# The experts' down slabs issued from ScalarE's DMA queue, up slabs kept on SyncE's

## The chip, the cores and the metric

The kernel runs on one core of a Trainium2 chip. The metric is device time in microseconds (us), the median of several runs. A profile is one further execution, recorded by the hardware profiler. Engines are named as the profile names them: PE is TensorE (matmuls), PEld its weight loads, DVE VectorE, ACT ScalarE, POOL GpSimd and SP SyncE. SPq and ACTq are the queues from which SyncE and ScalarE issue transfers.

## The reference

Two blocks of two layers each, all in float32, on 256 tokens of width 1024. The first block mixes the tokens (attention, Fourier, gates) and then sends them through 16 experts, of which each takes the 32 tokens that score highest for it. In layer 0 this is done for two token sets (the latents and the context), in layer 1 for the latents alone.

```
def expert_choice_ffn(h, w_router, w_gate_e, w_up_e, w_down_e):
    B, N, _ = h.shape
    cap = CAPACITY_FACTOR * N // N_EXPERTS
    aff = jax.nn.softmax((h @ w_router).astype(jnp.float32), axis=-1)
    top_aff, top_idx = lax.top_k(aff.transpose(0, 2, 1), cap)
    ...
    a = jnp.einsum("becd,edf->becf", xg, w_gate_e)
    u = jnp.einsum("becd,edf->becf", xg, w_up_e)
    out = jnp.einsum("becf,efd->becd", jax.nn.silu(a) * u, w_down_e) * top_aff[..., None].astype(h.dtype)
    return jnp.zeros_like(h).at[bidx, top_idx].add(out)
```

Each expert has three matrices of 1024 x 1024 floats (4 MB each), so the 32 expert passes read 32 x 12 MB of weights. The second block (three kinds of attention and a cross attention, two layers) has no experts.

## The kernel before

All weights go through one ring in SBUF, `ring`, with four slots of 2 MB (`RING = 4`). `slab_plan` lists the slabs in the order in which TensorE uses them. For an expert these are six: parts 0 to 3 ("up slabs") hold two row blocks of w_gate_e and two of w_up_e, in two transfers of 1 MB; parts 4 and 5 ("down slabs") hold four row blocks of w_down_e each, in one transfer of 2 MB. `loads` gives the transfers of a slab. An engine program is written by hand for each engine, and an engine runs its instructions in that order.

SyncE walks through the whole plan (line 711 on). Before slab i it waits until `slab_used` has reached i - 3, that is, until the slab that lay in the same slot has been used; then it issues the transfers, which count up the slot's semaphore. TensorE waits for that semaphore (`slab_wait`), multiplies, and counts up `slab_used` (`last_release`, line 840).

In `experts` TensorE does, for each expert, the four up slabs (line 1109; in layer 0 for two token sets, `ns = 2`, in layer 1 for one). Then come, from the fifth expert on, matmuls that add earlier results to the tokens (line 1093). Then it turns the product (line 1123), which needs ScalarE's copy of the up product out of PSUM (line 1391). ScalarE's sigmoid (line 1396) and VectorE's products (lines 1840, 1845) must be done before the two down slabs (line 1136). Behind the first down slab TensorE gathers rows for a later group of experts (line 1015), which ScalarE copies (line 1354); behind the second it turns weights (line 1026), which ScalarE copies too (line 1360). ScalarE's own program for an expert is: copies of the up product, sigmoids, row copies, weight copy. It issues transfers only at the start of the kernel (line 1443), 0.16 MB in all.

Of the kernel before, what the change touches and what calls it, by code (L numbers as in the profile page):

```python
# [33 lines left out]
RING = 4  # L34
# [90 lines left out]
def signal(name):  # L125

    if name in SHARED:
        return SHARED[name]
    base = name.replace("@0", "").replace("@1", "")
    return base, LAYER0[base] if "@1" in name else 0  # L130
# [8 lines left out]
def build(nc, a, out, ctx):  # L139
# [5 lines left out]
    def sem(name):  # L145
        name = signal(name)[0]
        if name not in sems:
            sems[name] = ctx.enter_context(nc.semaphore(name))
        return sems[name]
# [95 lines left out]
    def slot(i):  # L245
        return ring[:, (i % RING) * SLAB:(i % RING + 1) * SLAB]

    plan = slab_plan()
    where = {p: i for i, p in enumerate(plan)}

    def kcol(w, n0, n):
        return w.rearrange("(k p) n -> p k n", p=P)[:, :, n0:n0 + n]

    def loads(kind, l, s):

        if kind == "ada":
            return [(0, KC, COL, kcol(a["w_ada"][l], s * COL, COL))]
        if kind == "expert":
            e, part = s // 6, s % 6
            if part < 4:  # L260
                return [(c0, 2, D, a[name][l, e].rearrange("(k p) n -> p k n", p=P)[:, 2 * part:2 * part + 2, :])
                        for c0, name in ((0, "w_gate_e"), (2 * D, "w_up_e"))]
            return [(0, 4, D, a["w_down_e"][l, e].rearrange("(k p) n -> p k n", p=P)[:, 4 * (part - 4):4 * (part - 4) + 4, :])]
        if kind == "qkv":
            return [(0, KC, COL, kcol(a["w_in"][l], s * COL, COL))]
        if kind == "gate":
            return [(0, KC, COL, kcol(a["w_in"][l], MIX + (s % 3) * D + (s // 3) * COL, COL))]
        if kind == "branch":
            return [(0, 2, COL, kcol(a["w_br_fourier"][l], s * COL, COL)),
                    (2 * COL, 4, COL, kcol(a["w_br_global"][l], s * COL, COL)),  # L270
                    (6 * COL, 2, COL, kcol(a["w_br_window"][l], s * COL, COL))]
        if kind == "out":
            return [(0, KC, COL, kcol(a["w_out"][l], s * COL, COL))]
        if kind == "in2":
            return [(0, KC, COL, kcol(a["w_in_2"][l], s * COL, COL))]
        if kind == "out2":
            return [(0, KC, COL, kcol(a["w_out_2"][l], s * COL, COL))]
        if kind == "xq":
            return [(0, KC, COL, kcol(a["w_xq_2"][l], 0, COL))]
        if kind == "xkv":  # L280
            return [(0, KC, COL, kcol(a["w_xkv_2"][l], s * COL, COL))]
        return [(0, 4, D, kcol(a["w_xo_2"][l], 0, D))]
# [16 lines left out]
    slab_used = sem("slab_used")  # L299
# [411 lines left out]
    @block.sync  # L711
    def _(sp):
        for i, (kind, l, s) in enumerate(plan):
            if i >= RING:
                sp.wait_ge(slab_used, i - RING + 1)
            for c0, k, n, src in loads(kind, l, s):
                sp.dma_start(slot(i)[:, c0:c0 + k * n].rearrange("p (k n) -> p k n", k=k), src
                             ).then_inc(sem(f"slab_landed{i % RING}"), 16)
        sp.wait_ge(*at("result", 2))
        for t in range(2):  # L720
            sp.dma_start(out[0, t * P:(t + 1) * P, :], X[:, t, :]).then_inc(sem("stored"), 16)
        sp.wait_ge(*at("stored", 32))
# [517 lines left out]
    def _(act):  # L1240
# [71 lines left out]
        def experts(l):  # L1312
            ns = 2 - l
            order = tile_order(l)
            place = order.index
            turn_of = set_order(l).index
            log_and_exp()

            def square(t):
                n = place(t) + 1  # L1320
                act.wait_ge(*at(f"x_mid@{l}", n))
                act.activation(XN[:, t, :], X[:, t, :], ACT.Square, accum_out=st[:, SS + t:SS + t + 1]
                               ).then_inc(sem(f"n2@{l}_sq"), 1)
                act.wait_ge(*at(f"n2@{l}_var", n))
                act.activation(st[:, RS + t:RS + t + 1], st[:, VAR + t:VAR + t + 1], ACT.Ln
                               ).then_inc(sem(f"n2@{l}_ln"), 1)
                act.wait_ge(*at(f"n2@{l}_ln", n))
                act.activation(st[:, RS + t:RS + t + 1], st[:, RS + t:RS + t + 1], ACT.Exp, scale=-0.5
                               ).then_inc(sem(f"n2@{l}_rs"), 1)

            def modulated_tile(t):
                act.wait_ge(*at(f"n2@{l}_t0", place(t) + 1))
                s = t // 2
                for k in range(4):
                    ins = act.activation(HT[:, k, t * P:t * P + P], ps[6 if t == 3 else 4][:, k * P:(k + 1) * P], ACT.Identity,
                                         scale=SCL[:, l, 1, k, s:s + 1], bias=MODT[:, l, 24 + k, s:s + 1])
                ins.then_inc(sem(f"n2@{l}_ht0"), 1)

            def exps(s):
                act.wait_ge(*at(f"rmax@{l}", turn_of(s) + 1))  # L1340
                for t in range(2):
                    ins = act.activation(affinities(s)[:, t, :], ps[2 * s][:, t * E:(t + 1) * E], ACT.Exp,
                                         bias=soft_stat("neg", s)[:, t:t + 1],
                                         accum_out=soft_stat("sum", s)[:, t:t + 1])
                ins.then_inc(sem(f"rexp@{l}"), 1)

            pieces = [0]

            def rows_in(g, s, h):
                pieces[0] += 1  # L1350
                act.wait_ge(*at(f"gathered@{l}", pieces[0]))
                for kk in range(4):
                    k = 4 * h + kk
                    ins = act.activation(XGT[:, s, k, g * P:(g + 1) * P], ps[6 + h][:, kk * P:(kk + 1) * P], ACT.Identity,
                                         scale=SCL[:, l, 1, k, s:s + 1], bias=MODT[:, l, 24 + k, s:s + 1])
                ins.then_inc(sem(f"xgt@{l}"), 1)

            def weights_in(g, s, b, n):
                act.wait_ge(*at(f"gw_turned@{l}", n))
                act.activation(GW[:, s, g, :], ps[b][:, 0:SEQ], ACT.Copy).then_inc(sem(f"gw@{l}"), 1)  # L1360

            if l == 0:
                square(2)
                square(3)
                act.wait_ge(*at(f"mod@{l}", 2))
                modulated_tile(2)
                modulated_tile(3)
                exps(1)
            square(0)
            modulated_tile(0)  # L1370
            square(1)
            modulated_tile(1)
            exps(0)
            act.preload_act_table(ACT.Sigmoid)
            if l == 0:
                rows_in(0, 1, 0)
                rows_in(0, 1, 1)
            for m in range(2 * ns):
                act.wait_ge(*at(f"gmm@{l}_1", m + 1))
                act.activation(GB[:, m // 2, m % 2 * COL:(m % 2 + 1) * COL], ps[2 + m % 2][:, :], ACT.Copy  # L1380
                               ).then_inc(sem(f"grow@{l}_1"), 1)
            rows_in(0, 0, 0)
            rows_in(0, 0, 1)
            turned = 0
            for e in range(E):
                for s in range(ns):
                    m = e * ns + s
                    act.wait_ge(*at(f"up_done@{l}", m + 1))
                    if e:
                        act.wait_ge(*at(f"gu_turned@{l}", m - ns + 1))  # L1390
                    act.activation(GU[:, s, :], ps[s][:, :], ACT.Copy).then_inc(sem(f"gu_read@{l}"), 1)  # L1391
                for s in range(ns):
                    m = e * ns + s
                    act.wait_ge(*at(f"gu_turned@{l}", m + 1))
                    gate = ps[2 + s][:, :].rearrange("p (c n) -> p c n", c=4)[:, :, 0:2 * CAP]
                    act.activation(EG[:, s], gate, ACT.Sigmoid).then_inc(sem(f"eg@{l}"), 1)
                if e < 12:
                    for s, h in gather_pieces(l, e % 4):
                        rows_in(e // 4 + 1, s, h)
                if weight_set(l, e % 4) >= 0:  # L1400
                    turned += 1
                    weights_in(e // 4, weight_set(l, e % 4), 7 - e % 2, turned)
# [659 lines left out]
```

## Time and profile before

| | us |
|---|---|
| median of 3 runs | 2778.69 (2778.27 to 2779.12) |
| time of the profiled execution | 2783.78 |
| its span, first to last instruction | 2781.9 |
| PE busy | 2188.0 (79%) |
| PEld busy | 1056.5 (38%) |
| DVE busy | 737.7 (27%) |
| ACT busy | 455.0 (16%) |
| mean granted TensorE clock | 0.878 |
| TensorE in the experts of layer 0 | 645.45 to 1135.57 in the trace |
| TensorE in the experts of layer 1 | 1466 to 1947.67 in the trace |

The page divides the span into 40 slices of 69.5 us and gives for each the busy share of an engine in tenths, the granted TensorE clock and what the DMA engines moved. A share over the whole span is a mean of stages with different limits, so the stages have to be read one by one: by windows, by the order of instructions in time, and by what an engine waited for. In the order of time a row is a start, a duration and an operation; the number in brackets is how long the engine had been idle, and for what.

### The profile page before, as it was taken

The numbers are of one execution on the slowest core, as the hardware profiler recorded it, in microseconds if no ns is written. First come the engines' busy times: TensorE is split into PE (matmuls) and PEld (weight loads), VectorE is DVE, ScalarE is ACT, GpSimd is POOL, SyncE is SP. The second block draws the span as 40 slices with busy tenths as digits, with TensorE's granted clock in tenths as the row PEclk, the third lists the DMA queues.
The fourth block names the chain that finished last, engine by engine and source line by source line (L and its number), as shares of the span: only waits on it lengthen the run. The fifth ranks groups of instructions, "written<-read, shape, count | busy, mean of one in ns | idle before, by whom it ended". The sixth has DMA issues, their size and how long they took to land.

```text
span 2781.9 us, 30472 instructions
## 1 busy us (share of the span) xinstructions
PE 2188.0 (79%) x12882; PEld 1056.5 (38%) x12882; DVE 737.7 (27%) x1873; ACT 455.0 (16%) x1097; POOL 22.9 (1%) x44
## 2 busy tenths in 40 slices
PE   4997999888888888798976655555697679896686
PEld 3444544454333333354442121111244434334433
DVE  1030720342222222334140011111304731115622
ACT  1011700012101110115011000000103411013302
POOL 2000000000000000000000000000000000000000
PEclk8999999989999999999987798878896579995588
DMA  9136036416999999531328999999441022340010
GB/s 299 61 127 237 1 111 222 182 61 262 408 409 408 407 405 409 220 114 54 121 91 354 409 409 409 409 409 407 162 141 44 1 76 91 121 151 1 16 61 23
DMA packets 187333, 577.30 MB, mean 208 GB/s; under 512 B 7392, under 2 KB 7856, under 8 KB 187200
## 3 DMA queue, kind: packets, MB, share of 16 engines
q1 hardware_dynamic: 183936, 567.31, 52.9%
q0 software_dynamic: 2800, 7.89, 1.0%
q8 instruction: 104, 1.70, 0.3%
q14 instruction: 29, 0.24, 0.0%
q10 hardware_dynamic: 464, 0.16, 0.0%
HBM read 574.28 MB, written 1.05 MB: 207 GB/s over the span
## 4 chain that ended last, share of the span: by engine, by line
PE 36%; DMA 25%; issue 16%; DVE 8%; PEld 8%; PEldq 4%; ACT 3%; SPq 1%; POOL 0%; DVEq 0%; POOLq 0%
PE ps L831 16%; DMA ring<-w_up_e 15%; DMA ring<-w_down_e 7%; PEld ps L831 4%; PEldq L841 3%; PE ps L964 3%; PE ps L1109 2%; PEld ps L1136 2%; PE ps L921 2%; DMA ring<-w_ada 2%; PE ps L424 1%; DMA ring<-w_in 1%; PE ps L514 1%; PE ps L412 1%; PE ps L533 1%
## 5 line engine op out<-in xcount | busy, mean ns | idle before, releaser
L831 PE MATMUL ps<-ring,reg_a 128*128 128x512 f32 (+1 forms) x1632 | 710.7, 595 | 18.8 <-issue 8.2
L1109 PE MATMUL ps<-ring,reg_bc 128*32 128x512 f32 x3072 | 414.3, 678 | 181.9 <-DMA ring<-w_up_e 173.7
L831 PEld LDWEIGHTS ps<-ring,reg_a 128*128 128x128 f32 x1632 | 312.1, 193 | 412.8 <-issue 397.9
L1109 PEld LDWEIGHTS ps<-ring,reg_bc 128*32 128x32 f32 x3072 | 95.3, 117 | 476.2 <-DMA ring<-w_up_e 277.4
L1136 PE MATMUL ps<-ring,reg_bc 128*32 128x256 f32 x3072 | 182.8, 386 | 74.0 <-issue 42.7
L1136 PEld LDWEIGHTS ps<-ring,reg_bc 128*32 128x32 f32 x3072 | 104.1, 111 | 138.3 <-issue 55.6
L1827 DVE TENSOR_TENSOR reg_e<-ps,reg_e 128x512 f32<-128x512 f32 x48 | 33.0, 687 | 454.7 <-PE ps L1093 454.7
L1516 DVE COPY reg_bc<-ps 128x512 f32<-128x512 f32 (+1 forms) x33 | 22.3, 675 | 445.3 <-PE ps L831 445.3
L1391 ACT ACTIVATE reg_bc<-ps 128x512 f32<-128x512 f32 x48 | 28.7, 597 | 657.0 <-PE ps L1109 657.0
L1855 DVE COPY reg_a<-ps 32x256 f32<-32x256 f32 x192 | 80.7, 420 | 205.8 <-PE ps L1136 203.3
L412 PE MATMUL ps<-ident,tmp 128*128 128x128 f32 x160 | 50.3, 414 | 73.7 <-DVE tmp L635 47.4
L1269 ACT ACTIVATE reg_bc<-ps 128x512 f32<-128x512 f32 (+1 forms) x33 | 19.3, 584 | 440.7 <-PE ps L831 440.7
L921 PE MATMUL ps<-ring,reg_d 128*128 128x512 f32 x192 | 85.0, 603 | 4.0 <-DMA ring<-w_br_window 2.9
L964 PE MATMUL ps<-ring,reg_a 128*128 128x512 f32 x192 | 86.1, 607 | 1.8 <-DVE reg_e L1649 1.6
L814 PE MATMUL ps<-ident,reg_d 128*128 128x128 f32 x160 | 41.3, 413 | 54.9 <-DVE reg_d L1499 51.4
L797 PE MATMUL ps<-ring,ct 128*32 128x128 f32 x1536 | 53.4, 296 | 30.9 <-DMA ring<-w_ada 27.3
L424 PE MATMUL ps<-reg_bc,tmp 128*128 128x64 f32 (+1 forms) x320 | 70.8, 375 | 0.0
L424 PEld LDWEIGHTS ps<-reg_bc,tmp 128*128 128x128 f32 x320 | 70.1, 305 | 0.6
L412 PEld LDWEIGHTS ps<-ident,tmp 128*128 128x128 f32 x160 | 22.9, 193 | 114.4 <-DVE tmp L635 57.8
L1269 ACT ACTIVATE reg_e<-ps 128x512 f32<-128x512 f32 x36 | 21.5, 597 | 264.0 <-PE ps L831 263.9
L403 PE MATMUL ps<-reg_e 64*128 64x256 f32 (+1 forms) x128 | 60.3, 612 | 2.5 <-ACT reg_e L1418 0.9
L797 PEld LDWEIGHTS ps<-ring,ct 128*32 128x32 f32 x1536 | 46.0, 120 | 39.4 <-DMA ring<-w_ada 28.9
(276 smaller groups left out, 1982.1 us busy)
## 6 DMA issues: line engine op xcount, KB each, us to landing
ring<-w_gate_e SPq DMA_DIRECT2D x128, 1024.0 KB, 13.4
ring<-w_up_e SPq DMA_DIRECT2D x128, 1024.0 KB, 16.3
ring<-w_down_e SPq DMA_DIRECT2D x64, 2048.0 KB, 16.7
ring<-w_in SPq DMA_DIRECT2D x34, 2048.0 KB, 8.7
ring<-w_ada SPq DMA_DIRECT2D x24, 2048.0 KB, 15.7
ring<-w_out SPq DMA_DIRECT2D x8, 2048.0 KB, 8.5
ring<-w_xkv SPq DMA_DIRECT2D x4, 2048.0 KB, 7.8
ring<-w_br_global SPq DMA_DIRECT2D x4, 1024.0 KB, 8.0
```

The lines of the kernel that those rows point to most:

```text
L403: mm = pe.matmul(score_bank(i)[:, 0:u["nk"]], u["q"], u["k"], start=True, stop=True)
L412: mm = pe.transpose(ps[2 + j % 2][:, c * P:c * P + P], S2[j % 2][:, c * P:c * P + P], ident[:, :])
L424: mm = pe.matmul(ps[4 + j % 2][:, 0:w], PT[j % 2][:, c * P:c * P + P], u["v"][c], start=(c == 0), stop=(c == n - 1))
L797: mm = pe.matmul(ps[6 + s % 2][32 * j:32 * j + 32, 0:P], CT[:, k, :], w[:, k, j * P:j * P + P], start=(k == 0), stop=(k == KC - 1))
L814: mm = pe.transpose(ps[4 + 2 * s + k % 2][:, t * P:t * P + P], src[:, 2 * s + t, k * P:k * P + P], ident[:, :])
L831: mm = pe.matmul(ps[b][:, c0:c1], lhs(t, k), w[:, k, c0:c1], start=(q == 0), stop=(q == len(chunks) - 1))
L841: pe.drain().then_inc(slab_used, 1)
L921: mm = pe.matmul(ps[4 + n % 4][:, :], OT[:, k, t * P:t * P + P], w[:, k, :], start=(k == k0), stop=(k == k1 - 1))
L964: mm = pe.matmul(ps[t][:, :], HT[:, k, t * P:t * P + P], w[:, k, :], start=(k == 0), stop=(k == KC - 1))
L1109: mm = pe.matmul(ps[s][32 * j:32 * j + 32, :], XGT[:, s, 2 * q + k, e * CAP:(e + 1) * CAP], w[:, j // 2, k, (j % 2) * COL:(j % 2 + 1) * CO ...
L1136: mm = pe.matmul(ps[4 + s][32 * j:32 * j + 32, 0:SEQ], HE[:, s, k, q * CAP:(q + 1) * CAP], w[:, k, j * SEQ:(j + 1) * SEQ], start=(q == 0 a ...
L1855: ins = dve.tensor_copy(OE[r:r + CAP, e // 4 % 2, s, j * SEQ:(j + 1) * SEQ], ps[4 + s][CAP * j:CAP * (j + 1), 0:SEQ])
```

## The change

SyncE leaves out parts 4 and 5 of every expert. ScalarE issues them, at the head of its program for that expert, each behind a wait for the same count of `slab_used`. Slots, semaphores and sizes stay as they are.

```
     def _(sp):
         for i, (kind, l, s) in enumerate(plan):
+            if kind == "expert" and s % 6 >= 4:
+                continue
             if i >= RING:
                 sp.wait_ge(slab_used, i - RING + 1)
...
             rows_in(0, 0, 1)
             turned = 0
             for e in range(E):
+                for part in (4, 5):
+                    i = where[("expert", l, 6 * e + part)]
+                    act.wait_ge(slab_used, i - RING + 1)
+                    for c0, k, n, src in loads("expert", l, 6 * e + part):
+                        act.dma_start(slot(i)[:, c0:c0 + k * n].rearrange("p (k n) -> p k n", k=k), src
+                                      ).then_inc(sem(f"slab_landed{i % RING}"), 16)
                 for s in range(ns):
                     m = e * ns + s
                     act.wait_ge(*at(f"up_done@{l}", m + 1))
```

SyncE's queue at the end of layer 1's experts, before the change: the last up slabs, the two down slabs of the last expert, and the first slabs of the second block (w_in_2).

```order
L717 DMA ring<-w_gate_e 128x2x1024 [waits slab_used]
L717 DMA ring<-w_up_e 128x2x1024
L717 DMA ring<-w_gate_e 128x2x1024 [waits slab_used]
L717 DMA ring<-w_up_e 128x2x1024
L717 DMA ring<-w_down_e 128x4x1024 [waits slab_used] x2
L717 DMA ring<-w_in_2 128x8x512 [waits slab_used] x8
```

The same place after it (the line is now 719):

```order
L719 DMA ring<-w_gate_e 128x2x1024 [waits slab_used]
L719 DMA ring<-w_up_e 128x2x1024
L719 DMA ring<-w_gate_e 128x2x1024 [waits slab_used]
L719 DMA ring<-w_up_e 128x2x1024
L719 DMA ring<-w_in_2 128x8x512 [waits slab_used] x8
```

The two down transfers are gone from this queue, and the next stage's slabs follow the up slabs directly; at the end of each earlier expert the next expert's up slabs do.

ScalarE's queue in the experts of layer 0, before: two copies of the up product (`up_done`), two sigmoids, the row copies, the weight copy, and the next expert's copies.

```order
L1391 ACTIVATE reg_bc<-ps 128x512 [waits gu_turned,up_done] x2
L1396 ACTIVATE reg_bc<-ps 128x256 [waits gu_turned] x2
L1354 ACTIVATE reg_bc<-ps,modt,scl 128x128 [waits gathered]
L1354 ACTIVATE reg_bc<-ps,modt,scl 128x128 x3
L1360 ACTIVATE reg_e<-ps 128x256 [waits gw_turned]
L1391 ACTIVATE reg_bc<-ps 128x512 [waits gu_turned,up_done] x2
```

The same place after it (1391 is now 1399, 1396 is 1404, 1354 is 1356, 1360 is 1362):

```order
L1399 ACTIVATE reg_bc<-ps 128x512 [waits gu_turned,up_done] x2
L1404 ACTIVATE reg_bc<-ps 128x256 [waits gu_turned] x2
L1356 ACTIVATE reg_bc<-ps,modt,scl 128x128 [waits gathered]
L1356 ACTIVATE reg_bc<-ps,modt,scl 128x128 x3
L1362 ACTIVATE reg_e<-ps 128x256 [waits gw_turned]
L1392 DMA ring<-w_down_e 128x4x1024 [waits slab_used] x2
L1399 ACTIVATE reg_bc<-ps 128x512 [waits gu_turned,up_done] x2
```

The two issues stand between the weight copy of one expert and the up product's copies of the next, each with its wait for `slab_used`.

## Rows read from the trace of the kernel before

**Rows 1.** The page's 40 slices: DMA busy in tenths, and the rate.
```profile
DMA  9136036416999999531328999999441022340010
GB/s 299 61 127 237 1 111 222 182 61 262 408 409 408 407 405 409 220 114 54 121 91 354 409 409 409 409 409 407 162 141 44 1 76 91 121 151 1 16 61 23
```
**Rows 2.** The page's queues (packets, MB, share) and issues (KB, us to landing).
```profile
q1 hardware_dynamic: 183936, 567.31, 52.9%
...
ring<-w_down_e SPq DMA_DIRECT2D x64, 2048.0 KB, 16.7
```
**Rows 3.** DMA views of 680 to 1120 us, and then of 1480 to 1940 us.
```profile
DMA packets 45970, 179.43 MB, mean 408 GB/s; under 512 B 2266, under 2 KB 2266, under 8 KB 45934
...
DMA packets 48288, 188.20 MB, mean 409 GB/s; under 512 B 2399, under 2 KB 2399, under 8 KB 48267
```
**Rows 4.** PE in order of time, one expert of layer 1.
```profile
1806.29 1.92 PE L1109 MATMUL ps<-ring,reg_bc 128*32 128x512 f32 x16 [1.88 <-DMA ring<-w_up_e]
1811.39 3.25 PE L1109 MATMUL ps<-ring,reg_bc 128*32 128x512 f32 x16 [3.18 <-DMA ring<-w_up_e]
...
1818.37 1.93 PE L1136 MATMUL ps<-ring,reg_bc 128*32 128x256 f32 x32 [1.90 <-issue]
1821.90 1.93 PE L1136 MATMUL ps<-ring,reg_bc 128*32 128x256 f32 x32 [1.59 <-DMA ring<-w_down_e]
```
**Rows 5.** SyncE's issues in order of time, one up slab of the same expert.
```profile
1823.94 0.37 SPq L717 DMA_DIRECT2D ring<-w_gate_e  x1
1824.35 2.31 SPq L717 DMA_DIRECT2D ring<-w_up_e  x1
```
**Rows 6.** PE in order of time, one expert of layer 0.
```profile
941.22 3.66 PE L1136 MATMUL ps<-ring,reg_bc 128*32 128x256 f32 x64 [1.93 <-issue]
...
947.19 3.66 PE L1136 MATMUL ps<-ring,reg_bc 128*32 128x256 f32 x64
951.14 11.13 PE L1109 MATMUL ps<-ring,reg_bc 128*32 128x512 f32 x96 [0.29 <-issue]
963.17 3.64 PE L1109 MATMUL ps<-ring,reg_bc 128*32 128x512 f32 x32 [0.90 <-DMA ring<-w_up_e]
...
971.97 3.66 PE L1136 MATMUL ps<-ring,reg_bc 128*32 128x256 f32 x64 [1.94 <-issue]
```
**Rows 7.** The chain that ended last, at the end of either layer's experts.
```profile
1119.46 3.64 PE ps L1109 x32
...
1945.69 1.98 PE ps L1136 x32
```
**Rows 8.** DMA view of 0 to 30 us; windows of 4 to 16, 36 to 48 us.
```profile
GB/s 0 0 71 137 360 410 418 421 401 396 390 397 376 375 372 403 369 388 390 391 391 382 353 324 166 27 87 46 169 158 275 244 166 109 89 163 255 240 384 363
...
q0 software_dynamic: 1579, 3.60, 49.6%
q1 hardware_dynamic: 2167, 4.37, 43.4%
...
ring<-w_ada SPq DMA_DIRECT2D x4, 2048.0 KB, 33.4
...
4.00:16.00 12.00, 0.89 (x6) 0.48 (x10) 0.67 (x4) 1.94 (x3) 12.00 (x22) 1.00 1.05 392
36.00:48.00 12.00, 6.92 (x134) 5.52 (x130) 0.94 (x5) 0.00 (x0) 0.00 (x0) 0.77 1.05 387
```
**Rows 9.** The chain around 772 us, and a window there (last: clock, DMA share, GB/s).
```profile
772.54 5.34 PE ps L1109 x32
...
773.00:774.00 1.00, 1.00 (x12) 0.36 (x8) 0.00 (x0) 0.00 (x0) 0.00 (x0) 0.52 1.03 410
```
**Rows 10.** Whom ScalarE waited for, in total, times, longest.
```profile
ACT reg_bc L1391 <- PE ps L1109: 657.0, 48, 29.5
```
**Rows 11.** SyncE's first issues for layer 0's experts, and the window behind them.
```profile
649.17 4.11 SPq L717 DMA_DIRECT2D ring<-w_down_e  x2
...
650.00:660.00 10.00, 9.79 (x92) 2.62 (x84) 0.00 (x0) 0.60 (x1) 0.00 (x0) 1.00 0.96 372
```

More of the change, by code:

```diff
@@ L713, in _ @@
         for i, (kind, l, s) in enumerate(plan):
+            if kind == "expert" and s % 6 >= 4:
+                continue
             if i >= RING:
@@ L1385, in experts @@
             for e in range(E):
+                for part in (4, 5):
+                    i = where[("expert", l, 6 * e + part)]
+                    act.wait_ge(slab_used, i - RING + 1)
+                    for c0, k, n, src in loads("expert", l, 6 * e + part):
+                        act.dma_start(slot(i)[:, c0:c0 + k * n].rearrange("p (k n) -> p k n", k=k), src
+                                      ).then_inc(sem(f"slab_landed{i % RING}"), 16)
                 for s in range(ns):
```

## The prediction

> **What bounds the kernel now.** I read the slices of the page first: two stretches of about 480 us, the experts of layer 0 and of layer 1, in which the DMA digit is 9 and the rate stays at 405 to 409 GB/s [rows 1]. The DMA view of each stretch says the same: 408 and 409 GB/s with one queue, q1, doing nearly all of it [rows 2, 3]. A slab is 2048 KB [rows 2] or 2.097 MB, so it takes 2.097 / 0.409 = 5.13 us, and an expert (six slabs) 30.8 us. In layer 1 TensorE starts on the slabs as they land: up slabs at 1806.29 and 1811.39, the second down slab at 1821.90, each start with a wait for DMA before it [rows 4]. In layer 0 TensorE has two token sets and is close to the bound too. From the start of the fourth up slab at 963.17 its loop is 8.80 us to the first down slab, 5.97 to the second, 3.95 to the next expert's first up slab, 11.13 for three up slabs, and some 0.3 of gaps: 30.2 us against 30.8 [rows 6]. So both stages are bound by bytes, with 0.6 us of room per expert in layer 0.
>
> What I call U0 to U3 are an expert's up slabs, D0 and D1 its down slabs. A slab is issued when the one four places ahead has been used: D0 when U0 is used, D1 at U1, the next expert's U0 at U2.
>
> **What the change removes, adds and moves.** No byte, matmul or activation goes. 64 transfers of 2 MB leave SyncE's queue for ScalarE's, with a wait for the same count of used slabs. SyncE never was the limit: an issue takes it 0.37 us, against 5.13 us per slab, though a second one can be held for 2.31 us when much is outstanding [rows 5]. Taking work from it gives 0.
>
> ScalarE gets 64 issues, 64 x 0.37 = 24 us if they cost there what they cost SyncE. ScalarE sat idle 657.0 us in front of the 48 copies of line 1391, waiting for matmuls [rows 10]. It blocks on the use of U0 and then of U1. Behind it in its queue stand the copies that wait for U3, two slabs or at least 7.4 us later, and the row and weight copies of the expert before, which stand ahead of the issues, wait for matmuls that TensorE runs before U0. So issue times hardly move, and even a hold of 2.3 us would be over before U3 has been used. Cost 0. If that cover were gone, 2.3 us x 32 experts = 74 us would be the bound.
>
> What changes is the **order in which the bytes are served**. Before, one queue serves slabs in the order in which they are used. Afterwards the down slabs stand in a queue of their own beside the up slabs. The only place in the trace where two queues are busy together is the start: in the first 30 us the software queue took 49.6% of the engines' time and q1 43.4%, and the first four 2 MB slabs took a median of 33.4 us to land [rows 8]. Neither queue waited until the other was empty; they shared about evenly. The total was not changed: 392 GB/s in 4 to 16 us with both, against 387 for q1 alone on rows of the same 2 KB in 36 to 48 us [rows 8]. I take an equal share for SyncE's and ScalarE's queues; their pair is not in this trace, so both extremes are rivals below.
>
> The page "DMA: Bandwidth & Descriptors" of the Trainium skill says in "Queues, rings and completion order" that each DMA engine goes round between its queue rows packet by packet; the rows above agree with that. By its section "Issuing engines are not separate DMA queues" alone, which says only that the transfers interleave on the same 16 engines and that issue time is saved, the sum would be 0.
>
> Take U0's landing as time 0 in layer 1. In the order of use the landings are 0, 5.1, 10.3, 15.4 (U3), 20.5 (D0), 25.6 (D1), 30.8 (next U0). With equal shares D0 arrives when U2 is nearly served; U3 then has half the bandwidth for its whole service and lands at 10.7 + 10.3 = 21.0, with D0 just ahead of it. D1 then shares with the next U0 and both are in at about 30.3 to 30.8. The next U1 has the engines to itself. So the period stays 30.8 us, but **U3 and D1 are in about 5 us later than in the order of use**, and the place of what they lose is taken by slabs that are not needed yet. Inside the run that costs nothing while the DMA engines have work, since they set the pace. It is paid once, at the end of each stage, where slabs of the next stage have been served ahead of D1.
>
> *Layer 1.* D1 of the last expert starts at 1945.69 and ends at 1947.67 [rows 7]. U3 landed 10.3 earlier, 1935.4. Afterwards U3 is at 1940.5; 6.98 us to D0 [rows 4], 2.3 to D1 and 1.93 for it give 1951.7. By D1's own landing, 1945.7 + 4.7 + 1.98 = 1952.3. Cost 4.6, between 0 (order of use) and 9.2 (both down slabs wholly ahead of U3).
>
> *Layer 0.* The end follows U3 of the last expert, 1119.46, by a chain of matmuls, not D1's landing [rows 7]. U3 is 5.1 later in the first experts; of this the TensorE loop of 30.2 against 30.8 gives nothing back, since the engines are still the pace, but TensorE late means slabs issued late. I take 4.5, between 0 and 5.1 for this term.
>
> *A thin margin in layer 0.* At U3's landing 9.8 us of D1 and next U0 and 5.1 us of U1 are unserved, 14.9 us. The next issue, U2, comes when D0 is used, 8.80 + 3.66 = 12.5 us later, and some 1.4 us pass until it moves bytes (an estimate: the first issue is at 649.2 and the rate then reads 372 GB/s over 650 to 660 us [rows 11]): 13.9. So the DMA engines stay busy with 1.0 us to spare. The waits for U3 grow to 4 or 5 us, and after a wait of 2.71 us at 772.54 that slab's matmuls took 5.34 instead of 3.64 us while the granted clock read 0.52, close to the lower of its two levels, 1.2 of 2.4 GHz [rows 9]. That is 1.7 us more than the margin allows by 0.7, so 16 x 0.7 = 11 us if it came at each expert. A late TensorE does not wait, and then keeps its clock, so I take 2 us, between 0 and 11.
>
> In layer 1 TensorE has 10 us of room per expert and its fourth slab already runs 3.25 us, most of it at half clock [rows 4]; 0. Everything outside the experts has the same queue as before: 0; slabs served early for the next stages are not waited for there, 0 to -1.
>
> Sum: 4.6 + 4.5 + 2 = +11. On the profiled execution, 2783.78 us (span 2781.9), that is 2795; the median of the runs is 5.1 lower, so 2778.7 + 11.1 = 2790.
>
> **The rivals.**
> 1. *Order kept.* The queues serve the older transfer first, or the descriptors come through one place in order. For it: long holds of the second issue on SyncE, up to 2.3 us here [rows 5], show that something behind the issue fills up. Against: the shared start [rows 8]. Then nothing moves: 2779. A late ScalarE, so that D0 is issued only when it is needed, would belong here as "the change does not do what it says", but its idle time [rows 10] speaks against it.
> 2. *Unequal shares.* If ScalarE's queue gets clearly more than half, U3 waits for D0 and D1. At the extreme only 10.3 us are unserved when U3 lands, against 13.9 needed, so the DMA engines stand still 3.6 us per expert of layer 0: 58 us, plus 10 and 9 at the ends, 2856. The point from which this decides is the 1.0 us of margin. With less than half for ScalarE's queue D0 and D1 come late instead, with a like loss. The starting shares of 49.6 to 43.4 are near equal, so I price the case at a third of the extreme: 2800 to 2820.
> 3. *Faster.* Two queues keep the engines better filled. For it: single slices of the first 30 us read up to 421 GB/s [rows 8] where one queue holds 409; against: slices that follow read 376, and the stretch as a whole 392. If 3% held, layer 1 would win 14 us and layer 0, held by the loop of 30.2, 16 x 0.6 = 9; less 11 for the order: -12, 2767. It decides from 2% more bandwidth on (-10 and -9 against +11).
>
> **How the numbers follow.** Forecast (equal shares, 2784 to 2797) 0.52, predicted 2790. Order kept 0.22 (2776 to 2782). Unequal 0.17 (2797 to 2830, a tail beyond). Faster 0.09 (2765 to 2773). About 0.2%, 5.6 us, is what a measurement of this kernel can tell from no change, so the bounds are 2773 and 2784. Slower: 0.52 less 0.03 on its edge, plus 0.17, 0.66. Same: 0.22 + 0.03, 0.25. Faster: 0.09. The range of 2776 to 2808 leaves out the faster case and the upper half of the unequal one.
>
> **What would show it.** In the profile of the changed kernel: q10 with some 134 MB; 409 GB/s in both stretches; down slabs landing before or with U3; in layer 1 a wait of 7 to 10 us in front of U3 and next to none in front of D0 and D1; ScalarE's copies of line 1391 late only by U3; experts' stretches 5 us longer each. Waits in front of each slab as even as before would show order kept; gaps in the DMA rate in layer 0 would show rival 2; a rate over 412 GB/s rival 3. I am wrong above all if the two queues do not share evenly.

## The result, and the profile after

The changed kernel takes 2793.43 us (median; 2786.11 to 2799.22), the kernel before 2778.89 us beside it. The ratio is 1.0049, 95% interval 1.0037 to 1.0062: 14.5 us slower. The prediction was 2790, slower by 11.

The profiled execution has a span of 2791.1 us. Its slices and queues, which answer to [rows 1] and [rows 2]:

```profile
DMA  9136035416999999531328999999441022340010
GB/s 298 64 138 221 1 114 218 181 61 270 408 405 409 391 408 396 216 120 61 108 103 317 408 409 409 409 404 408 168 151 60 0 75 91 119 142 11 15 60 23
...
q1 hardware_dynamic: 150144, 433.08, 40.6%
q10 hardware_dynamic: 34256, 134.39, 12.1%
...
ring<-w_down_e ACTq DMA_DIRECT2D x64, 2048.0 KB, 15.8
```

ScalarE's queue is q10, and it carries the 134 MB. In the experts of layer 0 two slices read 391 and 396 GB/s where all read 405 to 409 before. The next windows run from the first up matmul to the last down matmul of each layer, of the kernel before and then of the changed one (length, busy times, granted clock, DMA share, GB/s):

```profile
645.45:1135.57 490.12, 416.06 (x4478) 179.24 (x4478) 111.76 (x252) 52.10 (x119) 0.00 (x0) 1.00 1.01 403
1466.28:1947.67 481.39, 281.27 (x2238) 91.24 (x2238) 55.78 (x124) 25.85 (x59) 0.00 (x0) 0.81 1.02 406
```
```profile
646.20:1145.10 498.90, 423.58 (x4478) 180.74 (x4478) 111.70 (x252) 52.09 (x119) 0.00 (x0) 0.98 1.01 398
1477.00:1962.70 485.70, 267.50 (x2238) 92.00 (x2238) 55.80 (x124) 25.85 (x59) 0.00 (x0) 0.80 1.02 404
```

Layer 0 is 8.8 us longer, layer 1 4.3 us, 13.1 together. The two spans differ by 9.2 only, since the rest was 3.9 us shorter this time. What is left of the span, the same work in all kernels, came out between 1800 and 1812 us from one profiled execution to the next. So I judge the experiments by these two windows as well as by the medians. The windows of the kernel with all issues on ScalarE, below, came within 1 us of those before. With two queues a window repeats less well: the four rows of the table below in which layer 1 has the changed kernel's program give 485.7, 486.2, 487.9 and 489.9 us there.

One expert of layer 1 after the change, answering to [rows 4] (TensorE in order of time):

```profile
1810.20 3.95 PE L1111 MATMUL ps<-ring,reg_bc 128*32 128x512 f32 x32 [0.29 <-issue]
1818.01 3.61 PE L1111 MATMUL ps<-ring,reg_bc 128*32 128x512 f32 x16 [3.86 <-DMA ring<-w_up_e]
1828.41 3.53 PE L1111 MATMUL ps<-ring,reg_bc 128*32 128x512 f32 x16 [6.78 <-DMA ring<-w_up_e]
...
1835.68 1.93 PE L1138 MATMUL ps<-ring,reg_bc 128*32 128x256 f32 x32 [1.91 <-issue]
1838.18 1.93 PE L1138 MATMUL ps<-ring,reg_bc 128*32 128x256 f32 x32 [0.57 <-DMA ring<-w_down_e]
```

U0 and U1 run without a wait between them, U2 lands at 1818.01 and U3 10.40 us after it. That is a slab at half the rate: 10.3 us was the figure. Then the down slabs are nearly there. The queues' shares in 1816 to 1817 us (packets, MB, share of the engines):

```profile
q10 hardware_dynamic: 50, 0.20, 51.1%
q1 hardware_dynamic: 49, 0.20, 50.5%
```

**Where the DMA engines stand still.** In layer 0 some windows lose bytes. First two windows of 30 us; then, from the first of them, TensorE's rows for a U3 and a D0, and SyncE's issue of the next U2:

```profile
910.00:940.00 30.00, 26.70 (x288) 11.87 (x284) 7.52 (x16) 3.21 (x8) 0.00 (x0) 1.00 0.95 366
1060.00:1090.00 30.00, 23.27 (x244) 9.59 (x248) 7.53 (x16) 1.96 (x4) 0.00 (x0) 0.89 0.97 378
```
```profile
906.02 5.34 PE L1111 MATMUL ps<-ring,reg_bc 128*32 128x512 f32 x32 [3.84 <-DMA ring<-w_up_e]
916.52 3.66 PE L1138 MATMUL ps<-ring,reg_bc 128*32 128x256 f32 x64 [1.94 <-issue]
...
920.25 0.37 SPq L719 DMA_DIRECT2D ring<-w_gate_e  x1
```

U3 waited 3.84 us, then ran at the lower clock, 5.34 us instead of 3.64; D0 was used at 920.2, and only then could the next U2 be issued. The rate read 289 GB/s in 918 to 920 us and 145 in 920 to 922. Against 409 GB/s, 30 us at 366 are (409 - 366) / 409 x 30 = 3.2 us of standing still, 30 us at 378 are 2.3, and a window of 30 us from 820 on with 402 gives 0.5, 6.0 together. In the second window it is the same: U3 waited 6.53 us and took 5.23 at 1063.86, and the rate read 277 and 127 GB/s in 1076 to 1080, around the issue of a U2 at 1077.88. By the same sum the kernel before loses 0.8 us.

**The end of the stage.** The last U3 of layer 0 and of layer 1, answering to [rows 7]:

```profile
1126.20 6.48 PE L1111 MATMUL ps<-ring,reg_bc 128*32 128x512 f32 x32 [3.32 <-DMA ring<-w_up_e]
...
1951.87 3.24 PE L1111 MATMUL ps<-ring,reg_bc 128*32 128x512 f32 x16 [7.08 <-DMA ring<-w_up_e]
...
1958.85 3.97 PE L1138 MATMUL ps<-ring,reg_bc 128*32 128x256 f32 x64 [1.90 <-issue]
```

In layer 0 U3 starts 480.0 us after the stage's first matmul; before it was 474.0 (1119.46 - 645.45). It then takes 6.48 us instead of 3.64: 6.0 + 2.8 = 8.8, all of the lengthening. In layer 1 U3 starts 474.9 us in, 5.7 later than before (1935.46 - 1466.28 = 469.2), and both down slabs run in one piece behind it without a wait for DMA. In this execution D1's landing is not what the end waits for. In two others, whose program for layer 1 is the same, TensorE did wait for it. These are the rows of the last D1 in the changed kernel's repetition and in the changed kernel with five more matmuls:

```profile
1954.37 1.94 PE L1138 MATMUL ps<-ring,reg_bc 128*32 128x256 f32 x32 [1.87 <-DMA ring<-w_down_e]
```
```profile
1965.02 3.64 PE L1142 MATMUL ps<-ring,reg_bc 128*32 128x256 f32 x32 [6.00 <-DMA ring<-w_down_e]
```

In the second of them the last U3 started 472.3 us in, only 3.1 later than before, and the stage took 489.9 us all the same. So the end of layer 1 has two ways to be late, U3's and D1's, and which one is taken changed from one profiled execution to the next.

### The profile page after: what moved, and what is told of

Same layout as the page of the kernel before. It is cut to its first block, busy times and chain, and to the rows that moved or that the text cites. A ratio compares the mean times of both kernels' runs of the same rounds, so it can differ in the third digit from the quotient of the medians.

```text
span 2791.1 us, 30472 instructions
## 1 busy us (share of the span) xinstructions
PE 2177.4 (78%) x12882; PEld 1057.7 (38%) x12882; DVE 737.5 (26%) x1873; ACT 454.8 (16%) x1097; POOL 22.9 (1%) x44
## 3 DMA queue, kind: packets, MB, share of 16 engines
HBM read 574.28 MB, written 1.05 MB: 206 GB/s over the span
## 4 chain that ended last, share of the span: by engine, by line
PE 40%; DMA 22%; issue 16%; DVE 8%; PEld 8%; PEldq 3%; ACT 3%; SPq 1%; POOL 0%; DVEq 0%; POOLq 0%; ACTq 0%
PE ps L833 16%; DMA ring<-w_up_e 13%; DMA ring<-w_down_e 6%; PE ps L1111 4%; PEld ps L833 4%; PE ps L966 3%; PEldq L843 3%; PE ps L923 2%; PEld ps L1138 2%; DMA ring<-w_ada 2%; PE ps L424 1%; DMA ring<-w_in 1%; PE ps L1138 1%; PE ps L514 1%; PE ps L412 1%
## 5 line engine op out<-in xcount | busy, mean ns | idle before, releaser
L1111 PE MATMUL ps<-ring,reg_bc 128*32 128x512 f32 x3072 | 403.7, 663 | 205.0 <-DMA ring<-w_up_e 190.4
L1111 PEld LDWEIGHTS ps<-ring,reg_bc 128*32 128x32 f32 x3072 | 96.3, 117 | 483.0 <-DMA ring<-w_up_e 252.0
L1524 DVE COPY reg_bc<-ps 128x512 f32<-128x512 f32 (+1 forms) x33 | 22.3, 675 | 443.0 <-PE ps L833 443.0
L1399 ACT ACTIVATE reg_bc<-ps 128x512 f32<-128x512 f32 x48 | 28.7, 597 | 672.2 <-PE ps L1111 672.2
L1848 DVE TENSOR_TENSOR reg_bc<-reg_bc,ps 128x256 f32<-128x256 f32 x48 | 19.9, 414 | 158.2 <-ACT reg_bc L1404 158.2
```

The costliest lines, as they stand in the source:

```text
L1111: mm = pe.matmul(ps[s][32 * j:32 * j + 32, :], XGT[:, s, 2 * q + k, e * CAP:(e + 1) * CAP], w[:, j // 2, k, (j % 2) * COL:(j % 2 + 1) * CO ...
```

## The experiments

Theory at the start: U3 of the last expert lands late because down slabs are served beside it, and in layer 0 the DMA engines stand still now and then. Rivals: ScalarE's issuing or a second queue costs time as such; the cost comes equally with each expert; or slabs of the next stage take D1's place. These are the stages of each kernel, by the windows described above (us; the last column is the ratio of the medians to the kernel before on the same chip):

| kernel | layer 0 | layer 1 | ratio, 95% interval |
|---|---|---|---|
| before | 490.1 | 481.4 | |
| changed | 498.9 | 485.7 | 1.0049 (1.0037 to 1.0062) |
| changed, once more | 498.7 | 486.2 | 1.0042 (1.0028 to 1.0056) |
| one queue, U3 and D0 swapped everywhere | 594.2 | 491.3 | 1.0402 (1.0387 to 1.0416) |
| all slabs issued by ScalarE | 490.2 | 482.2 | 1.0016 (1.0007 to 1.0025) |
| last expert only | 499.2 | 488.4 | 1.0056 (1.0042 to 1.0069) |
| all but the last | 493.2 | 483.0 | 1.0009 (1.0000 to 1.0018) |
| one queue, swapped in the last expert | 496.3 | 485.7 | 1.0031 (1.0021 to 1.0042) |
| last expert only, next stage held back | 500.0 | 491.1 | 1.0059 (1.0047 to 1.0071) |
| before, sums of layer 0 left out | 487.8 | 481.6 | 0.9994 (0.9982 to 1.0005) |
| changed, sums of layer 0 left out | 493.9 | 487.9 | 1.0046 (1.0032 to 1.0061) |
| changed, five more matmuls | 503.9 | 489.9 | 1.0042 (1.0029 to 1.0056) |

### Does ScalarE's issuing cost anything?

```
+                i0 = where[("expert", l, 0)] + 6 * e + 4
+                for part in range(3):
+                    issue(i0 + part)
...
+                issue(i0 + 3)
+                issue(i0 + 4)
...
+                issue(i0 + 5)
```

`issue` waits for the slot and issues the slab's transfers. D0, D1 and the next U0 stand ahead of the copies of the up product, the next U1 and U2 behind the sigmoids, the next U3 ahead of the weight copy; SyncE skips them all.

> All slabs that follow an expert's first four, up and down and the first four of the next stage, are issued by ScalarE, in the order of use, so that one queue again holds everything; the issues stand at the points of its program where the slot comes free. Theory (order of service): the time of before, 2776 to 2782, with ScalarE issuing 320 transfers instead of 64. Rival (ScalarE's issuing, with its holds, delays the copies, or issues late): slower than the change, 2793 or more, with five times its issues.

Both stages are back at the times of before, 490.2 and 482.2 us, with five times as many issues on ScalarE:

```profile
q10 hardware_dynamic: 107856, 402.84, 36.4%
q1 hardware_dynamic: 76544, 164.63, 16.5%
...
645.20:1135.40 490.20, 414.38 (x4478) 178.85 (x4478) 111.77 (x252) 52.19 (x119) 0.00 (x0) 1.00 1.02 403
1466.00:1948.20 482.20, 280.19 (x2238) 90.02 (x2238) 55.81 (x124) 25.89 (x59) 0.00 (x0) 0.83 1.02 406
```

The rival falls: what matters is that one queue holds the slabs in order, not whose queue it is. The median, 2785.70 us, is 0.16% above before, which the two stages don't explain; it lies outside the 2776 to 2782 expected, and stays open.

### One queue with the order that sharing produces: a kernel that failed its purpose

```
+        order = list(range(len(plan)))
         for i, (kind, l, s) in enumerate(plan):
+            if kind == "expert" and s % 6 == 3:
+                order[i], order[i + 1] = i + 1, i
+        for i in order:
+            kind, l, s = plan[i]
```

> All slabs stay on SyncE's one queue, but the first down slab of each expert is issued ahead of the fourth up slab. No second queue and nothing on ScalarE; what is copied from the change is that the fourth up slab (U3) lands one slab, 5.1 us, later. Theory (the order in which the bytes are served is the cause): the change's cost comes back without its queue, 2786 to 2795 against 2779 before; in layer 1 about 4 us longer, with U3's wait grown to 6 to 8 us and the down slabs already there. Rival 1 (a second queue, or ScalarE's issuing, costs time as such): 2779. Rival 3 of the prediction has nothing to say here.

114 us slower, nearly all in layer 0 (594.2 us), and not for the reason under test. SyncE runs in order. With D0 ahead of U3, U3's issue stands behind D0's wait for the use of U0, although its own slot came free with the use of the D1 before:

```profile
900.66 0.37 SPq L722 DMA_DIRECT2D ring<-w_down_e  x1
901.07 0.51 SPq L722 DMA_DIRECT2D ring<-w_gate_e  x1
...
900.00:905.00 5.00, 4.78 (x48) 1.25 (x44) 0.00 (x0) 0.00 (x0) 0.00 (x0) 1.00 0.66 196
...
935.00:940.00 5.00, 4.89 (x46) 1.44 (x50) 1.33 (x4) 0.38 (x1) 0.00 (x0) 1.00 0.08 32
```

By then everything issued had been served (32 GB/s in 935 to 940 us). 104 us over 16 experts is 6.5 us each. So this kernel says nothing of the order; it shows what it costs when an issue that is due waits behind one that isn't.

The same swap in the last expert alone:

```
+            if kind == "expert" and s == 6 * E - 3:
+                order[i], order[i + 1] = i + 1, i
```

> One queue, SyncE's, and nothing on ScalarE. Only in the last expert of each layer the first down slab is issued ahead of the fourth up slab (U3). Other than in the kernel with the swap in every expert, the DMA engines have three slabs waiting when SyncE stands at the down slab's wait, so they do not run dry. Theory (a late U3 of the last expert is what the change's cost at the end of a stage consists of): 5 us later and about 2 us of slower clock in layer 0, 4 us in layer 1, 2788 to 2793. Rival (a second queue, or ScalarE, is needed for the cost): the time of before, 2779.

```profile
1120.68 5.44 PE L1114 MATMUL ps<-ring,reg_bc 128*32 128x512 f32 x32 [6.59 <-DMA ring<-w_up_e]
```

The stages are 6.2 us longer in layer 0 and 4.3 in layer 1, the latter the same as the change's, and the median of 2791.88 us lies in the range expected. A late U3 alone, with one queue and no issue on ScalarE, is enough for a cost of this size at the end.

### Once at the end, or with each expert?

```
-            if kind == "expert" and s % 6 >= 4:
+            if kind == "expert" and s % 6 >= 4 and s // 6 == E - 1:
```

and, the other way round, `s // 6 < E - 1`, with ScalarE's loop cut in the same way.

> Only the last of the 16 experts of each layer has its down slabs issued by ScalarE, 4 transfers in all. Theory (the reordering is paid once, at the end of a stage, where slabs of the next stage are served first and U3 lands late): nearly all of the end costs, 4.5 in layer 1 and 4 to 5 in layer 0, 2786 to 2789. Rival (a cost per expert, each 14.5 / 32 = 0.45 us): +0.9, 2780.

> All experts but the last of each layer have their down slabs issued by ScalarE. Theory: layer 1 as before to 0.5 us, although U3 waits 7 to 10 us in 15 experts; layer 0 keeps what the standing still of the DMA engines costs, 3 to 5 us; 2781 to 2785. Rival (a cost per expert): 15/16 of 14.5, 2792.

Four moved transfers of 64 cost all of it: ratio 1.0056. The other 60 cost 0.0009, and in layer 1, where U3 waits long in each of 15 experts, 1.6 us. A cost per expert is ruled out. The last expert alone was expected to cost 7 to 10 us and costs 16 (9.1 and 7.0 in the stages), a miss; the two parts add up to more than the change. Its U3s:

```profile
1120.77 5.84 PE L1111 MATMUL ps<-ring,reg_bc 128*32 128x512 f32 x32 [5.08 <-DMA ring<-w_up_e]
...
1947.22 3.64 PE L1111 MATMUL ps<-ring,reg_bc 128*32 128x512 f32 x16 [6.76 <-DMA ring<-w_up_e]
```

In layer 0 U3 starts 481.0 us in, 7.0 later than before, and takes 2.2 us more at the lower clock. That is later than half the rate allows: the shares in 1109 to 1117 us of this kernel are not equal.

```profile
q10 hardware_dynamic: 615, 2.45, 76.7%
q1 hardware_dynamic: 213, 0.82, 25.8%
```

In layer 1 it is alike: 69.4% for q10 and 33.4% for q1 in 1936 to 1942 us, U3 7.9 later than before.

In the changed kernel D0 of the last expert is issued at 1115.47, when TensorE is already late, and U3 lands 10.7 us later; here D0 is issued at 1102.37, 18.4 us ahead of U3. In the changed kernel the DMA engines had stood still 5.2 us more than before, and U3 was 6.0 late; here they stood still 0.6 us by the same sum, no more than before, and U3 was 7.0 late. So, as far as these two show, lateness from standing still and lateness from sharing stand in for each other: the later TensorE is, the less of the down slabs is served ahead of U3.

### Are slabs of the next stage to blame?

The kernel with the last expert only, and in SyncE's loop:

```
+            ends = [where[("expert", d, 0)] + 6 * E for d in range(DEPTH)]
+            if i in ends:
+                sp.wait_ge(slab_used, i)
+            elif i >= RING and i - 1 not in ends and i - 2 not in ends and i - 3 not in ends:
```

> As the kernel in which only the last expert of each layer has its down slabs issued by ScalarE, but SyncE holds the first four slabs of the next stage back until that expert's second down slab has been used. So no slab of the next stage is served before the last down slab. The prediction's step (the place of what the down slabs lose is taken by slabs not needed yet, and D1 lands late): most of the end cost of 15.7 us goes, 2782 to 2786. Second theory (the end cost is U3, late because D0 and D1 themselves are served beside it; D1's own landing is not waited for): nothing of it goes, 2792 to 2797.

Nothing goes: 2797.45 us, ratio 1.0059 against 1.0056, and neither stage is shorter (500.0 and 491.1 us against 499.2 and 488.4). SyncE issues the next slabs at 1143.74, when the stage is over, and U3 of layer 0 still lands late:

```profile
1125.58 5.57 PE L1114 MATMUL ps<-ring,reg_bc 128*32 128x512 f32 x32 [4.98 <-DMA ring<-w_up_e]
...
1143.74 10.36 SPq L722 DMA_DIRECT2D ring<-w_in  x4
```

That is 482.0 us into the stage, 8.0 late. So where the end follows U3, the step of the prediction that blamed the next stage's slabs falls; D0 and D1 themselves are what U3 is late for. TensorE waited for the last D1 in neither of these two kernels, so the pair says nothing of the executions in which it did. There the step may hold. In the kernel with five more matmuls q1 moved some 1.1 MB of the next stage's slabs in 1952 to 1960 us, beside D0 and D1, and 1.07 MB more in 1960 to 1964, while TensorE stood waiting for D1: 2.2 MB or 5.3 us at 409 GB/s (an estimate), against a wait of 6.00. Nobody held them back in that kernel.

### The margin in layer 0

Both the kernel before and the changed one are run once more without the sums of the first twelve experts in layer 0, that is, without four matmuls per expert ahead of the down slabs and without VectorE's part of them (not shown):

```
+                    if l == 0 and turn < 3:
+                        pe.sem_inc(sem(f"scatter@{l}"), 1)
+                        continue
```

> The kernel before, with the adding of the first twelve experts' results to the tokens left out in layer 0 (the four matmuls per expert of 1.96 us in all between the fourth up slab and the down slabs, from the fifth expert on, and VectorE's products and sums for them). The way from the fourth up slab to the use of the first down slab is about 2 us shorter. Layer 0 is bound by DMA in either theory, so only the last expert's 2 us are won there: its experts take 488 instead of 490 us.

> The changed kernel with the same left out. Theory (in layer 0 a margin of 1 us between the bytes that are unserved and the next issue decides whether the DMA engines stand still): with 2 us more margin the gaps in the DMA rate go, and layer 0 is longer than in the kernel before without these sums by the end cost alone, 5 to 7 us instead of 8.9. Rival (the dips have another cause, such as the two queues themselves): dips of the rate to 360 or less stay, 9 us.

The stages came out as expected, 487.8 and 493.9, a difference of 6.1 us. The gaps did not go: windows of 30 us in the second kernel read 389, 398, 377 and 381 GB/s, together 6.7 us of standing still. So this pair came out neither as the theory (no gaps) nor as the rival (9 us). The reason stands in TensorE's rows:

```profile
999.77 6.50 PE L1114 MATMUL ps<-ring,reg_bc 128*32 128x512 f32 x32 [4.87 <-DMA ring<-w_up_e]
```

With less to do, TensorE waits longer for U3 (4.87 us), and the matmuls behind the wait take 6.50 us instead of 3.64. From U3's start to the next issue of U2 it is 13.1 us (1012.86), 1.1 less than in the changed kernel's case above (14.2), not 2. So the prediction's account of the margin is not shown by this pair: the 2 us were partly given back by the clock, and whether a fixed margin of 1 us decides stays open. What the rows do show is that, in the places looked at, the rate drops around the issue of a U2 that waited for TensorE's late use of D0.

### The clock

```
+                    if q == 3 and e == E - 1 and l == 0:
+                        pe.wait_ge(*at(f"hid@{l}", e * ns))
+                        for _ in range(5):
+                            pe.matmul(ps[2][:, 0:COL], ident[:, :], mask[:, 0:COL], start=True, stop=True)
```

> The changed kernel, and in front of the wait for the last expert's fourth up slab (U3) in layer 0 TensorE runs five more matmuls of 128x512 (about 3 us, into a bank that nobody uses then; their result is not read). They fit into the wait of 3.3 us. Theory (of the 8.9 us in layer 0, 2.8 are U3's matmuls at the lower clock, 6.48 instead of 3.64 us, because of the wait before them): U3 takes 3.6 to 4 us, and layer 0's experts are 2 to 3 us shorter than in the changed kernel, although TensorE has more to do; in all 2 to 3 us less, too little to be told by the medians alone. Rival (the clock falls for another reason, or its cost lies beside other work): layer 0 as in the changed kernel or longer.

> The changed kernel once more, on the same chip as the one with the added matmuls, to see how far its stages repeat. Theory (late U3 at both ends plus the standing still of the DMA engines in layer 0): layer 1 longer by 4 to 5.5 us than before, layer 0 by 7 to 11, with some windows of 30 us in layer 0 in which the rate is 360 to 400 GB/s, not necessarily the same ones. Rival (a cost that is the same each time for each expert): no such windows, equal lengthening of both layers.

```profile
1127.41 4.55 PE L1105 MATMUL ps<-mask,ident 128*128 128x512 f32 x10
1131.90 3.64 PE L1115 MATMUL ps<-ring,reg_bc 128*32 128x512 f32 x32
```

The added matmuls fill the wait (4.55 us, more than the 3.3 that it had been) and U3 takes 3.64 us. From the end of U2 to the end of the stage it is 20.7 us (1127.31 to 1148.01), against 22.3 in the changed kernel (1122.88 to 1145.17) and 22.6 in its repetition. The whole stage is nevertheless 5 us longer, 503.9, against what was expected: the DMA engines stood still for 12.5 us in earlier experts, in which nothing was altered (windows of 30 us at 392, 371, 330 and 372 GB/s), against 6.0 in the changed kernel. 6.5 more and 1.6 less are 4.9; measured 5.0. So the stage did not become shorter, as had been forecast; the theory's 1.6 us are seen only in the rows at its end. The repetition has its gaps at other places (394, 377 and 386 GB/s) and a stage of 498.7 us. The first runs of the changed kernel spread over 13 us and those of the kernel before over 3, which would go with this, but beside the later experiments the kernel before spread over 15 us too, so the spread is no proof.

## Why the prediction was right

- *Bound by bytes; room of 0.6 us per expert in layer 0.* Right: no experiment made a stage shorter than before, but for the 2.3 us at the end where the sums were left out.
- *Two queues share evenly, and the total stays.* Right in the changed kernel's experts (51.1 to 50.5%, U2 to U3 in 10.40 us; 409 GB/s where nothing stands still), which settles rivals 1 and 3. Not as a rule: 76.7 to 25.8% over 8 us in the kernel with the last expert only, and in the changed kernel itself 91.9 to 10.4% over the 4 us before the last U3 of layer 0 (1122 to 1126). Nor is it a rule for bytes: when q1 moved the next stage's slabs in packets half as large, both queues moved 272 packets in 1942 to 1946 us of the repetition, but q10 1.05 MB and q1 0.56. Of rival 2 only its mechanism came, in small measure.
- *ScalarE: 0.* Right. Its idle time in front of the copies grew from 657.0 to 672.2 us, and all slabs on its queue cost the stages nothing.
- *Layer 1: 4.6.* Measured 4.3 in the profiled execution, but 4.8, 6.5 and 8.5 in the three other profiled executions with the same program for layer 1. That it came within 0.3 is in part luck. Of the two ways to the sum, U3's holds here: 5.7 late where 5.1 was said, and 11.0 us behind it where 11.2 was. D1's landing was not waited for in this execution; it was in two of the others, by 1.87 and 6.00 us. Holding back the next stage's slabs gained nothing where U3 decides, and was not tried where D1 does.
- *Layer 0: 4.5 for the end and 2 for the margin.* Measured 8.8, so here the sum was too small. U3 was late by 6.0 and ran 2.8 us longer at the lower clock in the last expert, a price that the sum had only in the margin's term. The engines stood still 5.2 us more than before, where 2 (0 to 11) had been taken. The margin of 1.0 us was itself too wide: by [rows 11] 372 GB/s over 650 to 660 us is 0.9 us lost behind 650, 1.7 after the issue and not 1.4, which leaves 0.7. But standing still and the end's lateness are not added, as the pair of last and all but last shows (9.1 and 3.1 against 8.8).
- Sum: 11.1 forecast, 13.1 in the stages, 14.5 in the medians. The difference of the last two is within what the rest of the span varies by, 1800 to 1812 us.

## What to carry to other kernels

In these two stages, bound by the bytes, a second DMA queue brought nothing: it changed only which transfer landed first, and what was needed first landed later. Ask which transfer the end of the stage waits for and what is served beside it; moving four transfers of 64 cost as much here as moving all. With few ring slots a late landing also delays the next issues, so keep on one queue what is used in order, and let no issue that is due stand behind a wait for one that isn't.

## What the runs showed of the hardware

- Two queues of the same kind shared at 50 to 50 where both had slabs of experts (51.1 to 50.5% in 1816 to 1817 us), but also at 77 to 26 for 8 us. Why is open.
- Where the packets differed in size, the packets were shared evenly and the bytes were not: in 1942 to 1946 us of the repetition 272 packets each, 1.05 MB on q10 and 0.56 MB on q1. The queue with the larger packets had two thirds of the rate.
- A transfer issued by ScalarE at 1812.20 moved its first bytes only after 1815 (1813 to 1815 us show q1 alone), 2.8 us or more, where 1.4 had been estimated from an idle start. With SyncE's slabs waiting at that moment, it may stand behind them before it reaches its own queue; not tested.
- In layer 0 a wait of 3.3 to 6.6 us in front of U3 was followed by 1.6 to 2.9 us of lost time at the lower clock, the longest wait not by the largest loss (6.59 us, then 1.8); in the kernel with the wait filled, none.

```profile
1812.20 2.40 ACTq L1392 DMA_DIRECT2D ring<-w_down_e  x2
...
q1 hardware_dynamic: 212, 0.81, 101.6%
```
